# A block inverse that starts from a stored, masked product and a permutation matrix

## The reference, cut to what matters

```python
def step(S, inp):
    d_t, k_t, v_t, kk_t, a_t = inp[:5]
    sa = jnp.einsum("bhvk,bhk->bhv", S, -kk_t)
    S = (S * d_t[:, :, None, :] + sa[..., None] * (kk_t * a_t)[:, :, None, :]
         + v_t[..., None] * k_t[:, :, None, :])
    out = jnp.einsum("bhvk,bhk->bhv", S, inp[5]) if emit else None
    return S, out
```

## Time and profile before

| what | us |
| --- | --- |
| median of 3 runs | 2811.43 (2810.41 to 2815.81) |
| the profiled execution, its span | 2808.7 |
| the scan within it | 684 |
| TensorE busy, products / weight loads | 2512.4 / 1935.4 |
| VectorE, ScalarE, GpSimd busy | 1519.4, 1099.4, 735.1 |

### The profile page before, as it was taken

How to read it: one execution, slowest core, us unless ns; L and a number is a source line. 1 busy time by engine, 2 the same in 40 slices (tenths; PEclk the granted TensorE clock), 3 DMA queues, 4 the chain that set the end, 5 groups by cost and what they waited for, 6 DMA issues and landing times. The chain is left out here.

```text
span 2808.7 us, 66348 instructions
## 1 busy us (share of the span) xinstructions
PE 2512.4 (89%) x28704; PEld 1935.4 (69%) x28704; DVE 1519.4 (54%) x2491; ACT 1099.4 (39%) x1771; POOL 735.1 (26%) x422
## 2 busy tenths in 40 slices
PE   7998899999889995888888887889999999898997
PEld 5776577777667784777777776768788655475666
DVE  4744589863652213556666663344542466525975
ACT  4633321152453433455545543334422344323133
POOL 2422301422212225555545551100000000032132
PEclk9999999999899996999999999989999999998998
DMA  4224344434335531111111100633522100044431
GB/s 159 83 68 135 128 135 124 122 105 162 116 125 183 201 122 59 43 43 55 38 54 54 32 15 26 240 129 103 159 79 86 57 0 1 11 173 139 137 109 68
DMA packets 90286, 272.63 MB, mean 97 GB/s; under 512 B 13584, under 2 KB 14608, under 8 KB 89872
## 3 DMA queue, kind: packets, MB, share of 16 engines
q1 hardware_dynamic: 73104, 229.25, 25.6%
q10 hardware_dynamic: 16896, 39.16, 4.0%
HBM read 203.01 MB, written 36.70 MB: 85 GB/s over the span
## 5 line engine op out<-in xcount | busy, mean ns | idle before, releaser
L375 PE MATMUL ps<-h_parts_conv,w_parts_one 128*128 128x512 f32 x3168 | 579.8, 343 | 16.9 <-DVE h_parts_conv L361 13.7
L375 PEld LDWEIGHTS ps<-h_parts_conv,w_parts_one 128*128 128x128 f32 x3168 | 492.4, 190 | 107.5 <-issue 24.1
L375 PE MATMUL ps<-scratch_scan 64*64 64x64 f32 (+1 forms) x16704 | 383.1, 234 | 96.2 <-issue 56.1
L375 PEld LDWEIGHTS ps<-scratch_scan 64*64 64x64 f32 x16704 | 345.9, 137 | 139.5 <-issue 105.8
L372 ACT ACTIVATE scratch_scan<-ps 128x384 f32<-128x384 f32 x560 | 238.4, 495 | 331.7 <-PE ps L375 180.3
L443 POOL TENSOR_TENSOR w_parts_one<-ring,w_parts_one 128x1024 fp32r<-128x1024 f32 x83 | 208.2, 2509 | 581.4 <-ACT w_parts_one L372 581.3
L375 PE MATMUL ps<-h_parts_attn,w_parts_rwkv_out 128*128 128x512 f32 (+1 forms) x1536 | 329.2, 373 | 4.6 <-DVE h_parts_attn L369 4.6
L375 PEld LDWEIGHTS ps<-h_parts_attn,w_parts_rwkv_out 128*128 128x128 f32 x1536 | 263.2, 189 | 64.0 <-issue 9.4
L443 POOL TENSOR_TENSOR w_parts_rwkv_out<-ring,w_parts_rwkv_out 128x1024 fp32r<-128x1024 f32 x31 | 74.6, 2409 | 812.5 <-ACT w_parts_rwkv_out L372 812.5
L369 DVE SCALAR_TENSOR_TENSOR scratch_conv<-scratch_conv,vec 128x512 f32<-128x512 f32 (+1 forms) x408 | 252.6, 691 | 0.2
L372 ACT ACTIVATE w_parts_rwkv_out<-ring 128x1024 fp32r<-128x1024 f32 x104 | 109.5, 1056 | 344.0 <-PE ps L375 325.8
(11 more groups left out here) (219 smaller groups left out, 3263.6 us busy)
## 6 DMA issues: line engine op xcount, KB each, us to landing
ring<-in_weights SPq DMA_DIRECT2D x311, 512.0 KB, 3.7
rwkv_spill<-scratch_conv ACTq DMA_DIRECT2D x64, 384.0 KB, 2.3
stream<-rwkv_spill SPq DMA_DIRECT2D x64, 384.0 KB, 3.6
scratch_conv<-scratch_conv SPq DMA_DIRECT2D x120, 103.1 KB, 2.2
scratch_conv<-scratch_conv SPq DMA_DIRECT2D x120, 67.4 KB, 2.0
x_spill<-stream ACTq DMA_DIRECT2D x16, 384.0 KB, 2.5
kept_gate<-scratch_attn ACTq DMA_DIRECT2D x64, 64.0 KB, 2.6
y_spill<-scratch_scan SPq DMA_DIRECT2D x8, 384.0 KB, 2.5
```

Source lines behind the costliest of these rows:

```text
L375: return nc.tensor.matmul(o, l, r, start=start, stop=stop)
```

## The change

The start of the inverse isn't computed again from its factors. GpSimd multiplies the stored A by the mask of 2x2 blocks into `PQ` (`pair_blocks`, one operation of 128x768 a unit, placed behind `bonus_weights` and ahead of the masks of levels 0 and 1). What is stored is A transposed; inside a 2x2 block of a strictly triangular matrix a transposition is the exchange of the rows in pairs and of the columns in pairs. TensorE exchanges the rows by two products with a permutation matrix `swap` (128x128, 384 columns each), now placed behind Q4. VectorE exchanges the columns by reading PSUM in the order 1, 0, 3, 2, ... while it adds the identity (`p_start`, now behind `next_state` 10; `p_diagonal` is gone). What waited for `p_started` now waits until both of these additions have read their banks. The constants lose one mask of 64 columns and gain `swap` with 128.

```diff
--- before.py
+++ after.py
@@ -59,7 +59,7 @@
 
 CT, NCONST = {}, 0
 for _n, _w in (("ident", 128), ("ones", 128), ("ones64", 128),
-               ("gla_mask", 128), ("ident2", 64), ("centre", 64), ("ident4", 32), ("inv_mask", 7 * 64), ("wkv_mask", 2 * 128)):
+               ("gla_mask", 128), ("ident2", 64), ("centre", 64), ("ident4", 32), ("inv_mask", 6 * 64), ("swap", 128), ("wkv_mask", 2 * 128)):
     CT[_n] = (NCONST, _w)
     NCONST += _w
 
@@ -81,7 +81,7 @@
     put("centre", ((s == t) - 1.0 / CH)[:, :64])
     put("ident4", (i % 32 == j)[:, :32])
     m = [((s // (2 * b) == t // (2 * b)) & (s // b != t // b))[:, :64] for b in (1, 2, 4, 8, 16, 32)]
-    m = [m[0] & (t < s)[:, :64], m[0] & (t > s)[:, :64], *m[1:]]
+    put("swap", i == (j ^ 1))
     put("inv_mask", np.concatenate(m, 1))
     w = []
     for strict, incl in ((s < t, s <= t), (s > t, s >= t)):
@@ -1835,9 +1835,6 @@
 
         identb = C("ident2").rearrange("p (o t) -> p o t", o=1).broadcast_to([P, HALFC, CH])
 
-        def first_mask(d):
-            return C("inv_mask", d * CH, CH).rearrange("p (o t) -> p o t", o=1).broadcast_to([P, HALFC, CH])
-
         def chunk_of(d, st):
             return (NCX + st) % NSTEP if d == 0 else NSTEP - 1 - st
 
@@ -1857,8 +1854,8 @@
         FILLS = (("WU", 2), ("WU", 3), ("WU", 0), ("WU", 1), ("P1", 0), ("P1", 1), ("BT", 0), ("BT", 1), ("MR", 2), ("MR", 3),
                  ("NP", 0), ("NP", 1), ("MR", 0), ("MR", 1), ("P2", 0), ("P2", 1), ("KT", 0), ("KT", 1), ("G", 0), ("G", 1), ("G", 2), ("G", 3), ("AV", 0),
                  ("AV", 1), ("P3", 0), ("P3", 1), ("VT", 0), ("VT", 1), ("KS", 0), ("KS", 1), ("G", 4), ("G", 5),
-                 ("A", 0), ("A", 1), ("RC", 0), ("RC", 1), ("BO", 0), ("BO", 1), ("P4", 0), ("P4", 1), ("AT", 0), ("AT", 1),
-                 ("RS", 0), ("RS", 1), ("P5", 0), ("P5", 1), ("PI", 0), ("PI", 1), ("O", 0), ("O", 1))
+                 ("RC", 0), ("RC", 1), ("BO", 0), ("BO", 1), ("P4", 0), ("P4", 1), ("AT", 0), ("AT", 1),
+                 ("A", 0), ("A", 1), ("RS", 0), ("RS", 1), ("P5", 0), ("P5", 1), ("PI", 0), ("PI", 1), ("O", 0), ("O", 1))
 
         def fill_unit(name, p):
 
@@ -1910,7 +1907,7 @@
             if n > 1:
                 pe.wait_ge(fill_read[b], n - 1)
 
-        p_started = sem("p_started")
+        pairs_masked = sem("pairs_masked")
         out_squared = sem("out_squared")
         (t_done, t_copied, ob_done, q_done, pq_ready, n_masked, chain_done, state_ready, scanned, e_ready, d_ready,
          kf_ready, kt_ready, bk_ready, b0_ready, a_ready, r_ready, kk_squared, kk_root, kk_ready, bon_added, bon_scaled, bon_ready,
@@ -1950,7 +1947,8 @@
             def p_turned(lv):
                 def job(w, e):
                     if lv == 0:
-                        pe.wait_ge(p_started, 2 * (w + 1))
+                        for a_half in range(2):
+                            pe.wait_ge(*read_at("A", w, a_half))
                     else:
                         pe.wait_ge(pq_ready, level(w, lv - 1, 1))
                     name = f"P{lv}" if lv else "PI"
@@ -2011,22 +2009,18 @@
                                 if (j, x, par) == (1, 1, 1):
                                     last.then_inc(*done_inc("G", w, 2 * jj + h))
 
-            def first_inverse(w):
-                for h in range(2):
-                    room_for(pe, "A", w, h)
-                o = [bank3(fill_bank("A", w, h)) for h in range(2)]
-                for j in range(HALFC):
-                    for par in range(2):
-                        for h in range(2):
-                            last = mm(o[h][HS[par], j, :], AR[w % 3][HS[h], 2 * j + par, 0, :], XX[HS[h], bk_plane(w), j, 0, par, :])
-                            if (j, par) == (HALFC - 1, 1):
-                                last.then_inc(*done_inc("A", w, h))
+            def first_inverse(w, e):
+                room_for(pe, "A", w, e)
+                pe.wait_ge(pairs_masked, w + 1)
+                first = fill_bank("A", w, e) * 512
+                mm(PS[:, first:first + HALFC * CH], C("swap"), PQ[w % 2][:, half(e), :].rearrange("p q t -> p (q t)")).then_inc(*done_inc("A", w, e))
 
             def inv_t(w, lv):
                 n = level(w, lv, 1)
                 pe.wait_ge(n_masked, n)
                 if lv == 0:
-                    pe.wait_ge(p_started, 2 * (w + 1))
+                    for e in range(2):
+                        pe.wait_ge(*read_at("A", w, e))
                 if n > 2:
                     pe.wait_ge(pq_ready, n - 2)
                 for j in range(HALFC):
@@ -2197,7 +2191,6 @@
                 at(products, "G", p, 2)
                 chain(p, 6)
                 Q(3)
-                at(first_inverse, "A", p)
                 chain(p, 7)
                 both(centred, "RC")
                 both(bonus_sums, "BO")
@@ -2207,6 +2200,7 @@
                 both(a_turned, "AT")
                 chain(p, 9)
                 Q(4)
+                both(first_inverse, "A")
                 both(square_sums, "RS")
                 chain(p, 10)
                 both(p_turned(5), "P5")
@@ -2312,21 +2306,19 @@
                     n = level(w, lv, h)
                     v.wait_ge(q_done, n)
                     if lv == 0:
-                        v.wait_ge(p_started, 2 * (w + 1))
+                        for e in range(2):
+                            v.wait_ge(*read_at("A", w, e))
                     else:
                         v.wait_ge(pq_ready, n - 2)
                     pq = PQ[w % 2][:, h::2, :]
                     vtt(pq, bank3(h), pq, ALU.add).then_inc(pq_ready, 1)
 
             def p_start(w):
-                for h in range(2):
-                    v.wait_ge(*done_at("A", w, h))
-                    vtt(PQ[w % 2][:, h::2, :], bank3(fill_bank("A", w, h)), first_mask(w % 2)).then_inc(*read_inc("A", w, h))
-
-            def p_diagonal(w):
-                for h in range(2):
-                    v.wait_ge(*read_at("A", w, h))
-                    vtt(PQ[w % 2][:, h::2, :], PQ[w % 2][:, h::2, :], identb, ALU.add).then_inc(p_started, 1)
+                ones = C("ident2").rearrange("p (o t u) -> p o t u", o=1, u=2).broadcast_to([P, HALFC, CH // 2, 2])
+                for e in range(2):
+                    v.wait_ge(*done_at("A", w, e))
+                    o = bank3(fill_bank("A", w, e)).rearrange("p q (t u) -> p q t u", u=2)[:, :, :, ::-1]
+                    vtt(PQ[w % 2][:, half(e), :].rearrange("p q (t u) -> p q t u", u=2), o, ones, ALU.add).then_inc(*read_inc("A", w, e))
 
             def normal_out(i):
                 v.wait_ge(rt_ready, i + 1)
@@ -2385,12 +2377,8 @@
                     next_state(w3, 6)
                 if two:
                     inverse_update(w2, 3)
-                if one:
-                    p_start(w1)
                 if three:
                     next_state(w3, 7)
-                if one:
-                    p_diagonal(w1)
                 if one and w1 % 2 == 1:
                     for e in range(2):
                         bonus_values(w1 // 2, e)
@@ -2404,6 +2392,8 @@
                     inverse_update(w2, 4)
                 if three:
                     next_state(w3, 10)
+                if one:
+                    p_start(w1)
                 if wc < NUNIT:
                     cumulate(wc)
                 if fill_unit("RC", p - 1) is not None:
@@ -2589,7 +2579,16 @@
         def scan_pool(gp):
 
             def maskb6(lv):
-                return C("inv_mask", (lv + 2) * CH, CH).rearrange("p (o s t) -> p o s t", o=1, s=1).broadcast_to([P, 3, 2, CH])
+                return C("inv_mask", (lv + 1) * CH, CH).rearrange("p (o s t) -> p o s t", o=1, s=1).broadcast_to([P, 3, 2, CH])
+
+            def pair_blocks(w):
+                for j in range(6):
+                    gp.wait_ge(*read_at("G", w, j))
+                if w >= 2:
+                    for e in range(2):
+                        gp.wait_ge(*done_at("P5", w - 2, e))
+                m = C("inv_mask", 0, CH).rearrange("p (o s t) -> p o s t", o=1, s=1).broadcast_to([P, HALFC, 2, CH])
+                nc.gpsimd.tensor_tensor(PQ[w % 2].rearrange("p (j s) t -> p j s t", s=2), XX[:, aa_plane(w), :, 0, :, :], m, ALU.mult).then_inc(pairs_masked, 1)
 
             def off_blocks(w, lv):
                 for e in range(2):
@@ -2656,6 +2655,7 @@
                 if one and w1 % 2 == 0:
                     bonus_weights(w1 // 2)
                 if one:
+                    pair_blocks(w1)
                     off_blocks(w1, 0)
                     off_blocks(w1, 1)
```

## The result

The changed kernel takes 2855.74 us (median of 4 runs, 2854.24 to 2856.41) against 2813.62 for the kernel before in the same runs: a ratio of 1.0143, 95% interval 1.0128 to 1.0159: 42 us more by the two medians, 40 by the ratio. Forecast were 17 us, with a range up to 2846. The sign and the place were right; the size was not. Two executions at a lower clock are left out of the ratios: one of e2_filled_wait (3678 us), and one of the kernel before (2971 us) among those that e5 to e8 are compared with.

A forecast was written before the change was run, and what follows sets the result against it. TensorE's own order of work was taken to set the scan's length, with GpSimd late at `grown_b` in odd periods. Terms: 22 + 1.9 + 0 + 4.2 - 11 = +17 us, 2828.4 on the median; range 2814 to 2846.

The forecast's parts named there:

- The new wait in odd periods: TensorE behind Q4 waits for `pair_blocks`, queued on GpSimd behind `grown_b`: 4.1 us in p = 7.
- `grown_b` was to gain 1.5 us: GpSimd, odd periods: `grown_b` starts 1.5 us earlier because VectorE's `normal_kk` can start at 1367.9 in place of 1369.4.
- From the start of the swap to PI, 2.9 us: TensorE's tail: swap 1.3, drain 0.2, chain 10 0.1, `next_state` 10 0.2, additions 1.0, signal 0.1, together 2.9 us.
- The odd periods' total: Periods 3 to 13: PI 4.0 us later on average, 24 us, less 2 for vanishing level-0 mask waits: 22.
- The instruction stream, -11 us: TensorE's stream, 88 instructions fewer a period: 7 us, plus 4 us of gaps falling into waits; bounds -3 and -22.
- Even periods, +4.2 for seven: `pair_blocks` costs no wait; channel sums, chain 10, outputs and PI move by 0.6 us in each of seven periods.
- First two periods, +1.9: p = 0: `pair_blocks` in front of the awaited level-0 masks, +1.9 us; p = 1: 0, bounds 0 and 1.9.
- Outside the scan, 0: The change touches nothing outside the scan; the constants' 64 more columns in one starting load are costed at nothing.
- The second rival: Scan: the stream gives nothing back, or the exchanged reading costs more; +28 to +37, 2839 to 2848 us; chance 0.20.

The follow-up runs named there:

- e2_filled_wait: Changed kernel with six products of constants issued in odd periods ahead of TensorE's wait for `pair_blocks`, the wait kept; 2847.5 us, ratio 1.0129.
- e5: As e1_pairs_early, with `first_inverse` moved from behind Q4 to before chain 9 and `p_start` ahead of `next_state` 10; 2818.4 us, ratio 1.0009.
- e8: As e5, with the level-0 masks also ahead of `grown_b` in odd periods; 2819.45 us, ratio 1.0023.
- Experiments 1 and 2: The runs e1_pairs_early (2815.94 us) and e2_filled_wait (2847.5 us), both edits of the changed kernel.
- e1_pairs_early: Changed kernel with `pair_blocks` between `grown_k` and `grown_b` in odd periods, instead of behind `grown_b`; 2815.94 us, ratio 1.0008 to the kernel before.
- Experiments 4 to 6: Kernel before, first inverse's 24 products replaced by two of 128x128 (ratio 0.9983), by four of 64x64 (1.0050), or issued twice (1.0055).
- e3: Kernel before with `pair_blocks` alone added on GpSimd, only the masks behind it waiting for it; 2830.78 us, ratio 1.0065.
- e9: Kernel before with GpSimd making the level-0 masks ahead of `grown_b` in odd periods instead of behind it; 2811.17 us, ratio 0.9984.

## Why the prediction was wrong in size

The forecast was +17 us, the profiled spans differ by 43.8. Of the 26 us between, 12 lie in the odd periods, 11 are the gain that was booked for the shorter instruction stream, and the rest is small terms.

Step by step, by the prediction's own terms:

- *The new wait in odd periods*: right in place, cause and length. 4.1 us were forecast for p = 7, TensorE's idle time there is 4.03; over the six periods it is 3.8 on the mean. `grown_b` was to gain 1.5 us of earlier start; the waits of L2622 fell from 84.2 to 76.7, 7.5 us over the seven odd periods that have one, 1.1 each.
- *From the start of the swap to PI, 2.9 us*: **this is the first step that failed.** It is 4.7 us in four of the six periods, 4.5 and 3.4 in the others. The sum took every duration from rows at a clock of 1.00. It had TensorE stand idle for 4 us and didn't ask what the clock would do. The clock is at its lower level (1.2 of 2.4 GHz) in a part of each of these six periods, 31 us in all; in p = 13 its mean is 0.69 over the 8.9 us from the swap on, and it was 1.00 in the same period before. Experiments 1 and 2 show the swap at 1.56 with no wait or a filled one, against 2.90 behind the empty one; even there the way to PI is 3.2 us and not 2.9. The trace of before held a warning: the first periods of the scan, full of waits, are where most of the scan's mean clock of 0.96 in the earlier trace rows comes from, since the two whole periods there are at 1.00.
- *The odd periods' total*: +22 forecast before any relief, +34.3 measured. e1_pairs_early's odd periods are 33.3 us shorter than the changed kernel's, 5.5 each: 3.8 of idle wait, 1.25 of swap, P5 and PI at the lower clock, and 0.5 that is not assigned. Of the 12 us above the forecast of 22 the clock is 7.5, and 2 are the 0.3 us by which 2.9 was too small anyway; the last 3 are not assigned.
- *The instruction stream, -11 us*: **the second step that failed**, and nearly as large. The gaps fell by 11.2 (57.5 to 46.3), as in the sum; no gain of time followed that a run shows. e1_pairs_early has 13.7 us less of gaps than the kernel before and no wait behind `grown_b`, yet its periods 3 to 14 are 8 us longer, with 12 us more of busy time: a relief of some 4 us isn't excluded, one of 11 isn't seen. In the even periods of the changed kernel, where no new wait stands, the length rose by 5.9 us where 4.2 less a share of the relief was forecast. That gaps which go are replaced by waits for other engines is a guess that no run here shows. Experiments 4 to 6 show that the term isn't proportional to instructions at all: between -5 and +14 us for much the same removal. The prediction scaled with the count; what the gaps follow is which instructions stand at a multiple of 256 of the stream. The value to take was 0, with both signs in the bounds; a loss should not have been left out.
- *Even periods, +4.2 for seven*: +5.9 for six, +5.0 with p = 2: right.
- *First two periods, +1.9*: +3.9. The wait in p = 0 is 7.3 us; how much of the difference is the clock was not separated.
- *Outside the scan, 0*: +4.2 ahead of it and -2.2 behind it. The same stretch ahead of the scan reads -1.4 to +4.1 in kernels made from the changed one (+2.7 in e1_pairs_early) and 0 to +2.4 in kernels made from the one before. So it isn't fixed by the change; what sets it is open.

The sum with what was measured: 34.3 + 5.9 + 3.0 - 1.6 + 4.2 - 2.2 = 43.6. The second rival, no relief from the stream, gave 2839 to 2848; even this is 8 us short, and the clock's 7.5 us are what it lacked as well. The forecast missed by 26 because it also booked the stream's -11.

That it isn't GpSimd's load as such is shown by e1_pairs_early, which has the same load and is at the level of the kernel before. That a later or earlier place in its queue counts in the old kernel too is shown by e3 (+17) and e9 (-5).

## What to carry to other kernels

An operation put at the end of an in-order queue inherits the lateness of whatever waits ahead of it: here one line, placed before instead of behind an unrelated wait, is worth some 40 us. When a new wait of several microseconds is placed in front of TensorE, price what follows at both clock levels, since every duration read from a busy stretch was taken at the upper one. And don't book a gain for a shorter instruction stream, even where the gaps in it are plain to see.

## What was not expected of the hardware

TensorE's granted clock fell to half at single waits of 3.2 to 4.0 us: in each of the six odd periods of the changed kernel (0.69 over the 8.9 us from the swap of p = 13 on), and nowhere in the twelve periods of e1_pairs_early. In the same periods of the kernel before it did so once, for 3.4 us. A full-array product of 384 fp32 columns, two records, then took twice as long (records 0.64 us apart, 0.32 at the full clock).

Gaps without a semaphore, up to 2.7 us, interrupt runs of small products: 44 to 80 us of the scan in fourteen versions of this kernel. Nearly all over 0.3 us lie a multiple of 256 records of TensorE's stream apart (45 of 46 in the changed kernel). Removing 80 instructions of a period's 2320 at equal work raised their sum from 57.5 to 79.7 us, with two periods then exactly 18 such blocks long; removing 88 with 0.6 us more work lowered it to 48.9. What sets the length of each gap is open.
